# A grouped-query attention whose value products run as plain fp32 matmuls, with transposed probabilities and values kept in fp32

## What is computed

```python
def attention(q, k, v):            # q (B, 512, 2, 4, 128); k, v (B, 768, 2, 128)
    ...
    def one_block(qi):
        s = jnp.einsum('bqhgd,bkhd->bhgqk', qi, k).astype(jnp.float32) * scale
        p = jax.nn.softmax(s, axis=-1).astype(v.dtype)
        return jnp.einsum('bhgqk,bkhd->bqhgd', p, v)
```

## Time and profile before

| | |
|---|---|
| median of 3 runs | 2750.49 us (2747.46 to 2756.77) |
| profiled execution, its own time | 2758.05 us |
| its span (first to last instruction) | 2756.4 us |
| PE busy | 2646.0 us, 96% of the span |
| DVE busy | 1828.0 us, 66% |
| ACT busy | 1148.3 us, 42% |

### The profile page before, as it was taken

One profiled execution on the slowest core, in us unless ns is written; L12 is line 12 of the kernel. 1 busy time (PEld: TensorE's weight loads), 2 busy tenths in 40 slices (PEclk: granted clock), 3 DMA queues, 4 the chain that ended last, 5 costly groups with the idle time before them and its releaser, 6 DMA issues. The chain is left out here.

```text
span 2756.4 us, 38568 instructions
## 1 busy us (share of the span) xinstructions
PE 2646.0 (96%) x15222; PEld 2230.9 (81%) x15222; DVE 1828.0 (66%) x2954; ACT 1148.3 (42%) x1930; POOL 101.3 (4%) x123
## 2 busy tenths in 40 slices
PE   7989899999999999999999999999999999999997
PEld 4868788899999878878999978788867777777776
DVE  5578836666666667777888873665566656666576
ACT  3255525333333334555555542322344333334343
POOL 0110001100000000000000010000010000000000
PEclk9999999999999999999999999999999999999999
DMA  6430113433333311012333314222222222222221
GB/s 234 147 135 16 31 46 106 156 114 107 114 101 108 100 46 46 24 48 75 99 109 111 105 63 143 83 86 90 87 71 85 82 84 79 87 69 87 79 86 47
DMA packets 67407, 247.03 MB, mean 90 GB/s; under 512 B 7521, under 2 KB 8033, under 8 KB 66529
## 3 DMA queue, kind: packets, MB, share of 16 engines
q1 hardware_dynamic: 52288, 188.42, 21.1%
q0 software_dynamic: 14800, 55.65, 6.1%
q10 hardware_dynamic: 144, 0.52, 0.1%
HBM read 242.32 MB, written 2.24 MB: 89 GB/s over the span
## 5 line engine op out<-in xcount | busy, mean ns | idle before, releaser
L2662 DVE TENSOR_TENSOR WL<-RAW,WH 128x1024 fp32r<-128x1024 f32 (+1 forms) x199 | 242.9, 1222 | 268.1 <-ACT WH L1945 267.7
L1003 PE MATMUL PS<-AB,BH 128*128 128x384 f32 (+1 forms) x1256 | 389.4, 310 | 3.8 <-DVE BL L2669 2.5
L1003 PE MATMUL PS<-HM,WH 128*128 128x512 f32 x968 | 389.4, 402 | 3.1 <-ACT V L2467 2.2
L1004 PE MATMUL PS<-AB,BH 128*128 128x384 f32 (+1 forms) x1256 | 387.3, 308 | 0.0
L1005 PE MATMUL PS<-AB,BL 128*128 128x384 f32 (+1 forms) x1256 | 387.3, 308 | 0.0
L1004 PE MATMUL PS<-HM,WH 128*128 128x512 f32 x968 | 382.6, 395 | 0.0
L1005 PE MATMUL PS<-HM,WL 128*128 128x512 f32 x968 | 382.4, 395 | 0.0
L1945 ACT ACTIVATE WH<-RAW 128x1024 fp32r<-128x1024 f32 (+1 forms) x199 | 209.5, 1054 | 304.7 <-PE PS L1005 297.4
L1003 PEld LDWEIGHTS PS<-AB,BH 128*128 128x128 f32 x1256 | 235.9, 188 | 9.4 <-DVE GATED L3185 4.8
L1004 PEld LDWEIGHTS PS<-AB,BH 128*128 128x128 f32 x1256 | 235.9, 188 | 1.3 <-issue 0.5
L1005 PEld LDWEIGHTS PS<-AB,BL 128*128 128x128 f32 x1256 | 235.9, 188 | 0.0
(11 more groups left out here) (457 smaller groups left out, 5477.6 us busy)
## 6 DMA issues: line engine op xcount, KB each, us to landing
RAW<-in_tiles SPq DMA_DIRECT2D x298, 512.0 KB, 3.5
MRAW<-in_mods POOLq DMA_DIRECT2D x80, 512.0 KB, 4.6
RAW_M<-in_tiles SPq DMA_DIRECT2D x34, 512.0 KB, 3.5
TB<-bias_rows POOLq DMA_DIRECT2D x16, 576.0 KB, 6.2
FIRST<-in_mods SPq DMA_DIRECT2D x8, 1024.0 KB, 17.7
X_M<-in_x SPq DMA_DIRECT2D x1, 2048.0 KB, 12.6
VN_GB<-in_gm_rows POOLq DMA_DIRECT2D x2, 1024.0 KB, 6.3
out_x<-X_M SPq DMA_DIRECT2D x8, 256.0 KB, 2.1
```

Source lines behind the costliest of these rows:

```text
L1003: pe.matmul(out_, wh, xh, start=first, stop=False, skip_group_check=True)
L1004: pe.matmul(out_, wh, xl, start=False, stop=False, skip_group_check=True)
L2662: dve.tensor_tensor(WL[:, s.mod(2), 0:width], RAW[:, s.mod(2), 0:width], f32(WH[:, s.mod(2), 0:width]), ALU.subtract).then_inc(tile_split[ ...
```

## The change

The transposed probabilities go to one fp32 buffer `PTG` and the values to one fp32 buffer `VG`, in place of a high and a low fp32r buffer each. ACT's copy now raises `pt_ready` and `gqa_v_read` itself; DVE's 64 subtractions for the probabilities and 3 for the values are gone. A value product is 6 plain fp32 matmuls in place of 18 fp32r matmuls. The buffers lie where the old ones lay.

```diff
-    VG = [place(f"VG{n}", [P, 6, 2, P], (96 + n * 6) * KB, F32R) for n in range(2)]
-    PTG = PTA
+    VG = place("VG", [P, 6, 2, P], 96 * KB)
+    PTG = place("PTG", [P, 2, 6, 2 * P], 108 * KB)
...
                 for b in range(6):
-                    mm = three(GQA_OUT, VG[0][:, b, v, :], VG[1][:, b, v, :], PTG[0][:, x % 2, b, :], PTG[1][:, x % 2, b, :], b == 0, b == 5)
+                    mm = pe.matmul(GQA_OUT, VG[:, b, v, :], PTG[:, x % 2, b, :], start=(b == 0), stop=(b == 5), skip_group_check=True)
                 mm.then_inc(o_done, 1)
...
                 act.wait_ge(gqa_v_done, step + 1)
-                copy(VG[0][:, 2 * step:2 * step + 2, :, :].rearrange("p b v n -> p (b v n)"), v_bank(step)).then_inc(gqa_v_hi, 1)
+                copy(VG[:, 2 * step:2 * step + 2, :, :].rearrange("p b v n -> p (b v n)"), v_bank(step)).then_inc(gqa_v_read, 1)
...
-            def pt_high_of(w):
+            def pt_taken(w):
...
-                    b, src = gqa_pt(w, PTG[0], part)
-                    copy(b, src).then_inc(pt_hi, 1)
+                    b, src = gqa_pt(w, PTG, part)
+                    copy(b, src).then_inc(pt_ready, 1)
...
-            def v_read(step):
...
-            def pt_low(w):
-                for part in range(2):
-                    dve.wait_ge(pt_hi, gqa_pts(w) + part + 1)
-                    hi, src = gqa_pt(w, PTG[0], part)
-                    lo, _ = gqa_pt(w, PTG[1], part)
-                    low(lo, src, hi).then_inc(pt_ready, 1)
```

More of the change, by code:

```diff
@@ L2420, in _ @@
                 j = 2 * pair + 2
-                pt_high_of(w)
+                pt_taken(w)
                 if w + 2 < GQA_UNITS:
@@ L3352, in _ @@
             dve.wait_ge(rows_loaded, 16)
-            def v_read(step):
-                dve.wait_ge(gqa_v_hi, step + 1)
-                hi, lo = [x[:, 2 * step:2 * step + 2, :, :].rearrange("p b v n -> p (b v n)") for x in VG]
-                low(lo, v_bank(step), hi).then_inc(gqa_v_read, 1)
             def query_parts(j):
@@ L3451, in _ @@
             query_turned(1)
-            v_read(0)
             scale_of_queries(0)
             query_low(1)
-            v_read(1)
             maximum(0)
@@ L3469, in _ @@
                     part_added(n - 1)
-                pt_low(w)
                 if w == 0:
-                    v_read(2)
                     split(At(STREAM["gqa_q"] + 3))
```

## The result

The changed kernel takes 2760.36 us (median of 20 runs, 2755.59 to 2763.88), the kernel before 2754.39 us (20 runs). The ratio is 1.0019, 95% interval 1.0012 to 1.0026: about 5 us slower, where +0.10% was forecast (the two medians lie 6.0 us apart). That is inside 0.3%, "same" by the bound of the prediction, and inside its range.

What follows compares the result with a forecast made beforehand. PE was taken to bound the kernel, busy 2646.0 of 2756.4 us, not DVE. The terms 5.4 + 1.4 - 1.75 - 2.2 gave +2.9 us: 2760.9 on the profiled execution, 2753.3 on the runs' median, range 2745 to 2762.

Steps and rivals of the forecast that it cites:

- twelve products on PE's path: Twelve of 16 value products stand where PE sets the time; each takes 0.45 us more as fp32: +5.4 us.
- from products 2 and 6 to the transposes two units on: Pairs 0 and 1, DVE's chain beside PE's work: +0.7 us each with the clock falling as before, +1.4 together.
- the same from product 10: Pair 2, up to transposes(24): the wait for DVE's low part shrinks until unit 24's scaling is done, -1.75 us.
- behind transposes(24): Transposes, product 11 and one unit's scores run at full clock after a shorter wait: 4.31 us for 6.48, -2.2 us.
- The 4/3 of the split product's time: Rival: each value product costs 2.97 us at full clock, +6.8 us in all, 2757.3 us; chance 0.05.
- the rival with exposed weight loads: Rival: fp32 weight loads aren't covered by 256 moving columns, a product takes 4.1 us: +25 us, 2775; chance 0.05.
- the 0.56 us wait: Transposes(14)'s wait for DVE goes, but is added to the 1.25 us in front of product 6: no gain.
- If it falls again in the same way: Pair 0, product 2 to transposes(8): with the clock again at half speed there, 10.0 us in all, +0.7.
- the first rival: The clock never falls in the stage; pairs 0 and 1 give -1.5 and -1.0: -1.1 us, 2749.4; chance 0.17.
- At full clock they take 0.57 and 1.06 plus 2.68 = 4.31.: Transposes, scores and product 11 behind the wait in front of transposes(24), at full clock: 4.31 us for 6.48.
- DVE's relief as a gain of its own: Rival: DVE's order sets most units, up to 1 us for each of 32: -20 us or so, 2730; chance 0.05.
- The clock falling at every root and again behind product 10: Rival: half clock in all three pairs and at product 11, +7.7 us, 2758.2; chance 0.15.

Runs made afterwards that it cites:

- the first trace: The changed kernel's first profiled execution, against the kernel before: it took 2763.05 us, the stage 187.0 us for 183.6.
- the relief alone: Changed kernel with 18 fp32r matmuls a product again, reading the high part for the low; subtractions stay gone: 1.0007 to the kernel before, stage 183.7 us.
- The late wait alone: Output projection's wait for product 11 moved from its first matmul to its sixth chunk; on the changed kernel 1.0001 to the kernel before, stage 184.1 us.
- two moves: Projection's wait for product 11 at its sixth chunk, `QRAW` copy ahead of the exponential at n = 2: changed kernel 0.9989, kernel before 0.9975.
- three moves: Projection's wait at its sixth chunk, `QRAW` copy and ACT's root ahead of their exponentials: changed kernel 0.9961, repeated 0.9956; kernel before 0.9981.
- the one with the early read: Changed kernel, projection's wait for product 11 at its sixth chunk, `QRAW` copy ahead of the exponential at n = 2: 0.9989, stage 177.0 us.

## Why the prediction was right, and where not

The time lies in the range and the class held, and the stage's difference in the profiles, 187.0 - 183.6 = +3.4 us, is near the sum of +2.9. But two of its four terms were wrong, by -2.3 and +2.9 us, and their errors cancel: that the sum came so near is luck.

| term | predicted | measured in the first trace |
|---|---|---|
| twelve products on PE's path | +5.4 | 12 x 0.44 = +5.3; what is left of 3.36 without the three below is +5.4 |
| from products 2 and 6 to the transposes two units on | +1.4 | +0.14 - 1.06 = -0.9 |
| the same from product 10 | -1.75 | 7.02 - 8.78 = -1.76 |
| behind transposes(24) | -2.2 | 7.15 - 6.48 = +0.67 |

**The product.** 0.45 us forecast, 0.44 measured, in every kernel that has fp32 products. The fp32 records elsewhere in the program gave the price: 0.216 us a record, 0.215 forecast. The 4/3 of the split product's time, 0.74 us more, is refuted, and the rival with exposed weight loads, +1.9 us a product, is as well. The four passes of true fp32 that the Trainium skill names in FP8 and Floating Point Precision, TensorE Precision Notes, agree with the two records (0.43 us); 4/3 does not come out because a split matmul takes 0.118 us and not a fourth of that, 0.108. The three `v_read` steps, put at nothing, cost nothing: from the first scores to transposes(0) it is 8.84 us before and 8.83 in the changed kernel.

**The roots.** The forecast that the 0.56 us wait only moves in front of the product was right: 2.00 us stand there, 1.8 forecast. The 0.2 us more are not the product's surplus, since with split products and the same relief the wait is 2.00 us too, and product 5 to product 6 takes 9.63 us as before. With fp32 products it takes 0.37 us more, most of the product's own price.

**"If it falls again in the same way".** It did not. In pair 1 the clock stayed up, and the stretch took 7.76 us, the 7.8 that the prediction gave for full clock; in pair 0 it was low for 3.4 us instead of 6.8 and cost 9.45 for the 10.0 forecast. The mechanism and both prices hold; which case comes was mis-guessed, in the direction of the first rival. The prediction's own sign of being wrong, more than 17 us or none at half clock, did not come up: it was 3.4 us.

**"At full clock they take 0.57 and 1.06 plus 2.68 = 4.31."** This is the step that failed. The clock did stay up, and for the reason given: product 11 takes 3.73 to 3.98 us in the three traces with 3.06 us of wait in front of transposes(24), and 2.23 to 2.41 in the nine others. But the matmul that ends the stretch waits for `o_read` of product 11, and the prediction had counted only PE's work. The chain that leads there, all of it on DVE and ACT:

```profile
1197.64 1.22 DVE L2662 TENSOR_TENSOR WL<-RAW,WH 128x1024 fp32r<-128x1024 f32 x1
1197.76 0.99 ACT L2369 ACTIVATE PROB<-PS,STAT,LN 128x768 f32<-128x768 f32 x1 [2.78 <-DVE STAT L3381]
...
1198.74 0.62 ACT L1945 ACTIVATE QG<-RG 128x512 fp32r<-128x512 f32 x1
...
1199.40 0.69 DVE L2669 TENSOR_TENSOR QG<-RG,QG 128x512 fp32r<-128x512 f32 x1 [0.53 <-ACT QG L1945]
...
1200.20 0.62 DVE L3388 TENSOR_SCALAR PROB<-PROB,STAT 128x768 f32<-128x768 f32 x1
...
1200.73 0.95 DVE L3377 TENSOR_REDUCE STAT<-PS 128x1 f32<-128x768 f32 x1
...
1201.91 0.99 ACT L2369 ACTIVATE PROB<-PS,STAT,LN 128x768 f32<-128x768 f32 x1 [1.79 <-DVE STAT L3381]
...
1202.89 0.37 ACT L1945 ACTIVATE GM<-PS 128x256 fp32r<-128x256 f32 x1
...
1203.30 0.42 DVE L2669 TENSOR_TENSOR GM<-PS,GM 128x256 fp32r<-128x256 f32 x1 [1.42 <-ACT GM L1945]
```

A weight split on DVE, then a query's low part, which waits for ACT's high part, which stands behind the exponential; scaling, maximum, the next exponential, the output's high part, its low part. In the trace before the same steps stand like this:

```profile
1195.15 1.21 DVE L2662 TENSOR_TENSOR WL<-RAW,WH 128x1024 fp32r<-128x1024 f32 x1
...
1200.44 0.38 ACT L1945 ACTIVATE GM<-PS 128x256 fp32r<-128x256 f32 x1 [0.56 <-PE PS L1005]
...
1200.86 0.42 DVE L2669 TENSOR_TENSOR GM<-PS,GM 128x256 fp32r<-128x256 f32 x1 [1.17 <-ACT GM L1945]
```

From the weight split to the output's low part it is 5.66 us now (1197.64 to 1203.30) and was 5.71 (1195.15 to 1200.86), with a pair of subtractions in between; but those 5.71 hold 0.56 us in which ACT waited for product 11, which ran at half clock until 1200.2 and hid the rest. Now DVE waits for ACT in the subtractions' place, and product 11 is done by 1199.9. The chain keeps its length while PE comes sooner, and the wait for DVE that was taken away in front of transposes(24) is thus mostly spent again 7 us later. That was tried from both sides: with the wait moved the stretch is 4.35 us, and the relief alone gains nothing with it and 4.5 us without it. With the clock as it was in the first trace and no such wait, the prediction's sum would have been 5.4 + 0.14 - 1.06 - 1.76 - 2.2 = +0.5 us; the missed wait, with its 2.9, makes +3.4 of it.

**The rivals.** DVE's relief as a gain of its own (2730 us) was wrong in size: with its way free it is worth about 4.5 us, not 20. The clock never falling (-1.1 us) describes all of the stage but 3.4 us in pair 0; its sum is off by the missed wait. The clock falling at every root and again behind product 10 (+7.7 us) is as far from the ratio's +5.2 us as the forecast is, and the case of 4/3 (+6.8) is nearer to it, but the traces show neither.

**What stays open.** The ratio of the 20 runs says +5.2 us, the two traces +3.4 and +4.9 in the stage. Outside it, where PE's programs are equal, the twelve traces take 2568.6 to 2576.1 us, so single traces can't settle a microsecond or two, and there is only one trace of the kernel before. The price of the early wait for product 11 rests on more: 2.6 to 3.1 us of waiting in the three traces that have the relief and that wait, none in the seven with the wait moved. The late wait alone was not run in the kernel before, where nothing waited at that place.

The whole times and the stages also rank the tuned kernels differently. With two moves the split products are faster by 0.14% (0.9975 and 0.9989), with all three the fp32 products are by 0.25% (0.9956 and 0.9981), while the stages are equal within 0.4 us both times. With three moves the runs' own clocks point to why: over the whole program the mean granted clock is 0.988 (median of 7 runs) with fp32 products and 0.985 (12 runs) with split ones, so it fell for less time in the rest of the program. The profiled executions can't show where, as the one with fp32 products is the slowest of its seven runs (2752.35 us) and the other one of the fastest of its twelve (2745.55). With two moves the clocks are equal to 0.001. What makes it so was not tried.

## What to carry to other kernels

- Replacing three split matmuls by one plain fp32 matmul took 2 x 0.216 us for 3 x 0.118 at 256 columns. It trades PE's time for that of the engines that make the parts, and pays only where those engines set the time; here PE does, in 12 of 16 places.
- When a wait is taken away, follow the other engines' chain past it to PE's next wait, and read off what that one was hidden by. A loop's end, or the first step of a new phase, is where it comes back.
- Put a wait at the operand that needs it, and an engine's short reads, for which PE waits, ahead of its long operations that nobody waits for yet. These moves were worth 9 us of stage with split products and 12 with fp32 ones, more than the change itself; of the whole time, 0.2% and 0.6%.

## What the runs showed of the hardware

- With matmuls of 512 columns, 0.23 us apart at 2.4 GHz, the same fp32r matmul stands 0.42 apart at 1.2 GHz: the lower clock costs 1.8 and not 2 times. A plain fp32 matmul does lose 2 times: in product 2 of the changed kernel its records of 256 columns stand 0.216 us apart at the upper level and 0.427 at the lower. At 512 columns a record takes 0.431 us at the upper clock.
- Where the clock falls is in part chance: after an identical wait of 2.64 us it fell in one execution and stayed up in another, and with the same three root waits of 2.0 us it fell at all three in the relief alone, at one in the changed kernel and at none in the one with the early read. In part it goes with the kernel's waits: it was low at product 11 in all three traces with a 3.06 us wait ahead of it. In the three traces without the `QRAW` and the long projection wait and with fp32 products it never fell in the stage (clock 1.00 in the table).
